# A recurrence's doubling inverse without identity products, its key norm in four columns, and sums of squares one tile behind

## The reference, cut to what matters

```python
def step(S, inp):                      # per head, state S of 64 x 64
    r_t, w_t, k_t, v_t, a_t, b_t = inp
    sa = jnp.einsum('bhij,bhj->bhi', S, a_t)
    S = S * w_t[:, :, None, :] + sa[..., None] * b_t[:, :, None, :] + v_t[..., None] * k_t[:, :, None, :]
    return S, jnp.einsum('bhij,bhj->bhi', S, r_t)
...
kk = (k * k_k).reshape(B, T, H, N)
kk = kk * lax.rsqrt(jnp.maximum(jnp.sum(kk * kk, axis=-1, keepdims=True), 1e-24))
y = wkv7_scan(r, decay, k, v, -kk, kk * a)
...
def rms_norm(x, g, eps=1e-6):
    y = x * lax.rsqrt(jnp.mean(x * x, axis=-1, keepdims=True) + eps)
    return y * g
```

## Time and profile before

| | |
|---|---|
| time, median of 3 runs | 3502.67 us (3501.64 to 3502.81) |
| the profiled execution, its own time | 3507.43 us |
| its span, first to last instruction | 3505.6 us |
| TensorE, VectorE, ScalarE, GpSimd busy | 3188.5, 1696.9, 1161.2, 142.9 us |
| mean granted clock of TensorE | 0.911 of full |
| chain that ended last: TensorE, VectorE, ScalarE, issue | 82%, 10%, 4%, 2% |

### The profile page before, as it was taken

The page is one execution under the profiler, slowest core; times in us unless marked ns, Lnnn a source line. Parts: engine busy times, 40 slices in busy tenths (PEclk is TensorE's granted clock), DMA queues, the critical chain, the costliest instruction groups (busy, mean ns, idle before and its releaser), DMA issues.

```text
span 3505.6 us, 38393 instructions
## 1 busy us (share of the span) xinstructions
PE 3188.5 (91%) x15360; PEld 2547.2 (73%) x15360; DVE 1696.9 (48%) x2759; ACT 1161.2 (33%) x1871; POOL 142.9 (4%) x145
## 2 busy tenths in 40 slices
PE   7999798888888889999999997779999879988997
PEld 6888476677777778887788885458888356877886
DVE  5434543455555554344743447755434345336235
ACT  3323133434443343233332233543223233323332
POOL 0000000112111100000000000000000000000000
PEclk9999898778776899999999998689999979997998
DMA  3333231000000033332233322013333410201231
GB/s 126 98 97 96 64 102 34 3 3 3 4 3 13 1 121 101 97 97 95 79 96 102 93 82 75 1 30 97 97 98 95 154 51 1 76 19 46 79 96 54
DMA packets 173895, 234.75 MB, mean 67 GB/s; under 512 B 14201, under 2 KB 111062, under 8 KB 173462
## 3 DMA queue, kind: packets, MB, share of 16 engines
q1 hardware_dynamic: 173718, 232.29, 21.5%
HBM read 228.05 MB, written 4.19 MB: 66 GB/s over the span
## 4 chain that ended last, share of the span: by engine, by line
PE 82%; DVE 10%; ACT 4%; issue 2%; DMA 1%; POOL 0%; SPq 0%; DVEq 0%; ACTq 0%
PE banks L796 60%; PE banks L1221 3%; PE banks L889 2%; PE banks L1215 1%; PE banks L927 1%; PE banks L951 1%; PE banks L1209 1%; PE banks L957 1%; PE banks L1161 1%; PE banks L955 1%; PE banks L901 1%; DVE diff_scores L2177 1%; DVE diff_small L2183 1%; PE banks L860 1%; PE banks L948 1%
## 5 line engine op out<-in xcount | busy, mean ns | idle before, releaser
L1756 DVE TENSOR_TENSOR weights_lo<-weights_raw,weights_hi 128x1024 fp32r<-128x1024 f32 (+2 forms) x393 | 473.1, 1207 | 1034.4 <-ACT weights_hi L1289 1033.2
L796 PE MATMUL banks<-operand_hi,weights_hi 128*128 128x512 f32 x2208 | 874.2, 396 | 35.6 <-DVE weights_lo L1756 20.9
L796 PE MATMUL banks<-operand_lo,weights_hi 128*128 128x512 f32 x2208 | 867.3, 393 | 0.0
L796 PE MATMUL banks<-operand_hi,weights_lo 128*128 128x512 f32 x2208 | 867.1, 393 | 0.0
L1289 ACT ACTIVATE weights_hi<-weights_raw 128x1024 fp32r<-128x1024 f32 (+2 forms) x393 | 407.9, 1041 | 1096.4 <-PE banks L796 1040.4
L796 PEld LDWEIGHTS banks<-operand_hi,weights_hi 128*128 128x128 f32 x2208 | 419.3, 190 | 130.9 <-issue 25.5
L796 PEld LDWEIGHTS banks<-operand_lo,weights_hi 128*128 128x128 f32 x2208 | 419.4, 190 | 89.5 <-issue 2.4
L796 PEld LDWEIGHTS banks<-operand_hi,weights_lo 128*128 128x128 f32 x2208 | 419.1, 190 | 88.8
L796 PE MATMUL banks<-hidden_ffn_hi,weights_hi 128*128 128x512 f32 x352 | 136.9, 389 | 0.0
L796 PE MATMUL banks<-hidden_ffn_lo,weights_hi 128*128 128x512 f32 x352 | 136.9, 389 | 0.0
L796 PE MATMUL banks<-hidden_ffn_mid_hi,weights_hi 128*128 128x512 f32 x352 | 136.9, 389 | 0.0
(11 more groups left out here) (517 smaller groups left out, 4700.8 us busy)
## 6 DMA issues: line engine op xcount, KB each, us to landing
weights_raw<-in_ffn_w_in_dram SPq DMA_DIRECT2D x352, 256.0 KB, 3.1
weights_raw<-in_ffn_w_out_dram SPq DMA_DIRECT2D x88, 512.0 KB, 3.7
weights_raw<-in_w_in_dram SPq DMA_DIRECT2D x36, 512.0 KB, 3.6
weights_raw<-in_rwkv_w_rkv_dram SPq DMA_DIRECT2D x24, 512.0 KB, 3.9
weights_raw<-in_w_mod_dram SPq DMA_DIRECT2D x24, 512.0 KB, 4.6
weights_raw<-in_w_kv_dram SPq DMA_DIRECT2D x16, 512.0 KB, 3.6
weights_raw<-in_rwkv_w_o_dram SPq DMA_DIRECT2D x8, 512.0 KB, 5.2
weights_raw<-in_diff_w_q_dram SPq DMA_DIRECT2D x8, 512.0 KB, 4.6
```

The costliest lines, as they stand in the source:

```text
L796: mm = nc.tensor.matmul(o, l, r, start=first and t == 0 and job["opens"], stop=last and t == 2, **skip)
L1756: nc.vector.tensor_tensor(ring_lo[0:p, u["slot"], 0:n, 0:w], ring_raw[0:p, u["ring"], 0:n, 0:w], f32(ring_hi[0:p, u["slot"], 0:n, 0:w]), A ...
```

## The change

Three things are changed.

**Inverse.** The tables of masks now contain the identity: `seed` holds minus the near pairs (the second one plus the identity), and `level` is the identity minus the old mask. GpSimd adds the identity to the first half of `L.mq` (the new event `mi`), so that the product in step `x` already contains the old inverse, and the masked product `L.xm` is the whole factor. The growth of a level is then a plain product, and all 13 identity products of an item are gone. ScalarE's copy to `L.mh` waits for `mi` instead of the masked pair. In `refine` VectorE forms twice the identity minus the product (it was ScalarE's copy), and signs move: `L.ar` is no longer negated; ScalarE and VectorE negate in copies that exist anyway.

**Key norm.** In `decay` the squares are now the stationary operand, two products with 2 moving columns each, which leaves tokens on the partitions and four numbers for each. Maximum, root and reciprocal are over four columns; VectorE then spreads them over 256 columns (`rk`), and TensorE turns the result with two transposes in the step `norm`, which wait for `rk`. VectorE's `keys` reads them from the bank.

**Sums of squares.** In the feed-forward layers, after the time mix and the attention, and after the last layer, VectorE's addition for tile k-1 (and the rest of `fed(k-1)`) stands behind the writing of tile k.

```diff
                 elif step == "decay":
                     b = bank("kk")
                     pe.wait_ge(*by_act.at(at("sq")))
-                    nc.tensor.matmul(ps[:, b, 0:HT], headsum[:, :], L.t[7], start=True,
-                                     stop=True).then_inc(*by_pe.by(at("kk")))
+                    for tb in range(2):
+                        mm = nc.tensor.matmul(ps[:, b, 2 * tb:2 * tb + 2], L.t[7][:, tb * P:(tb + 1) * P],
+                                              headsum[:, 0:P:HEAD], start=True, stop=True)
+                    mm.then_inc(*by_pe.by(at("kk")))
+                elif step == "norm":
+                    b = bank("rk")
+                    pe.wait_ge(*by_dve.at(at("rk")))
+                    for tb in range(2):
+                        mm = nc.tensor.transpose(ps[:, b, tb * P:(tb + 1) * P], L.t[7][:, tb * P:(tb + 1) * P], ident[:, :])
+                    mm.then_inc(*by_pe.by(at("rk")))
...
-                    nc.tensor.matmul(ps[:, b], identr, joined(L.inv_t), start=True, stop=False, skip_group_check=True)
                     pe.wait_ge(*by_dve.at(at(f"xm{lv}")))
                     for p in range(4):
-                        mm = nc.tensor.matmul(ps[:, b, p * P:(p + 1) * P], L.xm[:, p], L.inv_t[:, p], start=False,
-                                              stop=True, skip_group_check=True)
+                        mm = nc.tensor.matmul(ps[:, b, p * P:(p + 1) * P], L.xm[:, p], L.inv_t[:, p], start=True, stop=True)
                     mm.then_inc(*by_pe.by(at(f"t{lv}")))
                     b = bank(f"i{lv}")
-                    nc.tensor.matmul(ps[:, b], identr, joined(L.inv), start=True, stop=False, skip_group_check=True)
...
                 elif step == "norm":
                     act.wait_ge(*by_dve.at(at("n2")))
-                    nc.scalar.activation(L.t[7], L.t[7], ACT.Sqrt,
+                    nc.scalar.activation(L.sm[:, 12:16], L.sm[:, 12:16], ACT.Sqrt,
                                          bias=eps[:, EPS_NONE:EPS_NONE + 1]).then_inc(*by_act.by(at("root")))
                 elif step == "pairs":
-                    act.wait_ge(*by_dve.at(at("mq1")))
+                    act.wait_ge(*by_pool.at(at("mi")))
                     nc.scalar.activation(L.mh, L.mq[:, :, 0, :], ACT.Copy).then_inc(*by_act.by(at("mh")))
...
-                            if part:
-                                fed(k)
+                            if part and k:
+                                fed(k - 1)
+                    if part:
+                        fed(KC - 1)
...
-                    nc.vector.reciprocal(L.t[7], L.t[7]).then_inc(*by_dve.by(at("rn")))
+                    nc.vector.reciprocal(sm[:, 12:16], sm[:, 12:16]).then_inc(*by_dve.by(at("rn")))
+                    dve.wait_ge(*by_dve.at(at("rn")))
+                    nc.vector.tensor_copy(heads_(L.t[7]), sm[:, 12:16].unsqueeze(2).broadcast_to(
+                        [P, 4, HEAD])).then_inc(*by_dve.by(at("rk")))
...
+                    pool.wait_ge(*by_dve.at(at("mq1")))
+                    nc.gpsimd.tensor_tensor(L.mq[:, :, 0, :], L.mq[:, :, 0, :], i4, ALU.add).then_inc(*by_pool.by(at("mi")))
                     pool.wait_ge(*by_dve.at(at("sd1")))
                     nc.gpsimd.tensor_tensor(L.inv, f32(L.inv), i4, ALU.add).then_inc(*by_pool.by(at("inv")))
+                    pool.wait_ge(*by_pool.at(at("mi")))
                     nc.gpsimd.tensor_tensor(L.inv_t, L.mq[:, :, 0, :], seed[:, 1].unsqueeze(1).broadcast_to([P, 4, P]),
-                                            ALU.mult).then_inc(*by_pool.by(at("seed")))
-                    pool.wait_ge(*by_pool.at(at("seed")))
-                    nc.gpsimd.tensor_tensor(L.inv_t, f32(L.inv_t), i4, ALU.add).then_inc(*by_pool.by(at("invt")))
+                                            ALU.mult).then_inc(*by_pool.by(at("invt")))
```

More of the change, by code:

```diff
@@ L371, in step_of @@
                 return "d", int(use[1])
-            return {"kk": "decay", "rx": "refine", "nv": "refine", "full": "full", "w": "w", "bon": "gh", "gh0": "gh",
+            return {"kk": "decay", "rk": "norm", "rx": "refine", "nv": "refine", "full": "full", "w": "w", "bon": "gh", "gh0": "gh",
                     "gh1": "gh", "z": "z", "out": "out", "yt": "y"}[use]
@@ L376, in wkv_done @@
             act = (["za", "a", "g"] if half == 0 else []) + ["sq", "ep", "en", "ea", "root", "mh"]
-            dve = (["lw"] if half == 0 else []) + ["cs", "cl", "n2", "rn", "am", "k2", "kk", "ma", "ka", "mb",
+            dve = (["lw"] if half == 0 else []) + ["cs", "cl", "n2", "rn", "rk", "am", "k2", "kk", "ma", "ka", "mb",
                                                     "mk", "mr", "mq0", "mq1", "sd0", "sd1", "ml"]
@@ L381, in wkv_done @@
                 dve += [f"xm{lv}"] + (["nq0", "nq1"] if lv == 0 else [])
-            act += ["rx", "full", "w", "var", "std", "yl"]
-            dve += ["nv", "bonus0", "bonus", "gh0", "gh1", "z"]
+            act += ["full", "w", "var", "std", "yl"]
+            dve += ["rx", "nv", "bonus0", "bonus", "gh0", "gh1", "z"]
             dve += ["s0", "s1", "s2", "s3"] if half == 0 else ["s0", "s1", "s2"]
             dve += ["sum", "mean", "yc", "vsum", "rstd", "yn", "y1", "y"]
-            pool = ["b2", "k3", "inv", "seed", "invt", "g", "clear"] + (["sb0"] if half else [])
+            pool = ["b2", "k3", "mi", "inv", "invt", "g", "clear"] + (["sb0"] if half else [])
             return [u[0] for u in wkv_uses(half) if u[0] != "bx0"], act, dve, pool
@@ L967, in pe_program @@
                         for part in (L.mh, L.ml):
-                            mm = nc.tensor.matmul(ps[:, b, p * P:(p + 1) * P], part[:, p], L.inv[:, p], start=False,
-                                                  stop=True, skip_group_check=True)
+                            mm = nc.tensor.matmul(ps[:, b, p * P:(p + 1) * P], part[:, p], L.inv[:, p],
+                                                  start=part is L.mh, stop=part is L.ml)
                     mm.then_inc(*by_pe.by(at("rx")))
@@ L1909, in dve_program @@
             fence("rkv")
[L1910 to L1912 removed]
+            nc.vector.tensor_scalar(two_ident, ident[:, :], 2.0, None, ALU.mult).then_inc(*wkv_ready.by(0))
             dve.wait_ge(*wkv_ready.at(0))
@@ L2075, in add_and_feed @@
                                                         ALU.add).then_inc(*evac_d.by(job))
-                                add_square(stage, k, free)
+                                if k:
+                                    add_square(stage, k - 1, free)
+                            if bi:
+                                add_square(stage, KC - 1, free)
                         if bi:
@@ L2604, in tables @@
     near = (i // 2 == j // 2)
-    t["seed"] = f(np.concatenate([near & (i > j), near & (i < j)], 1))
-    t["level"] = f(np.concatenate([(i // (2 * s) == j // (2 * s)) & (i % (2 * s) >= s) & (j % (2 * s) < s)
+    unit = (i == j).astype(np.int32)
+    t["seed"] = f(np.concatenate([0 - (near & (i > j)), unit - (near & (i < j))], 1))
+    t["level"] = f(np.concatenate([unit - ((i // (2 * s) == j // (2 * s)) & (i % (2 * s) >= s) & (j % (2 * s) < s))
                                    for s in (2, 4, 8, 16, 32)], 1))
```

57 lines of the change are left out of this document (26 added, 31 removed).

## The result

The change is slower: 3545.0 us (median of 6 runs, 3530.8 to 3552.2) against 3502.7 us for the kernel before in the same comparison (6 runs, 3486.0 to 3518.5). The ratio is 1.0098, 95% interval 1.0069 to 1.0127, about 1%. The profiled execution of the change is the quickest of its six (3530.8 us, span 3528.9), so its trace shows less of the loss than the medians: 23 us of span against 42.

The account below looks back on a forecast made before the run. TensorE, 91% busy, was taken as the bound, in the recurrence in turn with short waits on other engines. Terms -63 + 19 + 17 - 8 - 1 + 9 = -27 us gave 3476 us, range 3440 to 3508.

Parts of the forecast that it names:

- Identity products: Recurrence, TensorE: removing 208 products of 128x512 against the identity, about 0.30 us each, saves 63 us.
- Key norm: Recurrence, step `norm`: TensorE newly waits before the two transposes; 1.2 us an item over 16 items, +19 us.
- GpSimd: Recurrence, before the first level: the new sum `mi` makes `inv` end later; 1.1 us an item, +17 us.
- Squares: Serial stage ends: sums of squares one tile behind shorten waits before products of ones and for weights, -8 us together.
- constants: Fewer constants and a shorter first chain: -1 us.
- The wait of 2.12 us for weights at 2119.74: TensorE waits for weights SyncE issues after the last tile is written; that tile would be written about 2 us earlier.
- The clock: Recurrence: TensorE's mean granted clock falls from 0.75 to 0.736, 479 us of busy time becoming 488, +9 us.
- My own signs of being wrong: Recurrence shorter by over 45 us or no shorter; no wait at the transposes; or a clock below 0.71.
- The third rival: Recurrence: long gaps in every item lower the clock to 0.70 instead of 0.736, 25 us more, 3501 us; chance 0.15.
- The fourth rival: Recurrence: the new wait costs its full 3.3 us in 16 items, +34, 3510 us, slower; chance 0.15.

Follow-up runs that it names:

- e2: The kernel before with the key norm alone changed, identity products kept: 3548.1 us, ratio 1.0093 to the kernel before.
- e1: The kernel before with the inverse part alone (no identity products, new tables, new GpSimd sum): 3535.5 us, ratio 1.0065 to the kernel before.
- e3: The kernel before with the sums of squares alone one tile behind: 3503.4 us, ratio 0.9969 to the kernel before.
- e11: The change with 288 discarded products ahead of the waits for key norm, square of the keys and first level: ratio 0.9771 to the kernel before.
- e6: The change with 8 discarded products ahead of each wait for the key norm, 128 in all: 3510.1 us, ratio 0.9992 to the kernel before.
- e5: The change with the norm's transposes three turns later, at step `keys`: 3520.7 us, ratio 1.0039 to the kernel before.
- e13: The kernel before with the change's squares and key norm, late transposes, identity products kept, 304 discarded products: 3411.2 us, ratio 0.9724 to the kernel before.
- e8: The kernel before with the change's squares and key norm, transposes late at step `keys`, identity products kept: 3484.2 us, ratio 0.9920 to the kernel before.
- e4: The change with a discarded 128x512 product in each of the 13 places per item of an identity product: 3550.3 us, ratio 1.0106 to the kernel before.
- e10: The change with late transposes and 160 discarded products ahead of the waits for square of the keys and first level: ratio 0.9775 to the kernel before.

## Why the prediction was wrong

Forecast 3476 us, range 3440 to 3508; measured 3545, on the other side.

- **Identity products, -63 us**: right at a constant clock. The work fell by 47 us by the product and by 51 by the clock intervals, where I counted 50, and 47 / 0.75 = 63.
- **Key norm, +19, and GpSimd, +17**: places and sizes of the waits were right (2.7 to 3.4 us at the transposes forecast, 3.1 measured; no more waits of 3.7 us at the level product). As idle time e2 shows +11 and e1 +18, the change +15: the two do not add up, and 36 was too much. For GpSimd I had kept 1.77 us for `inv`; it is 1.26, and `mi` 1.27, so `inv` should have ended hardly later. But e1's wait for GpSimd before the first level still grew by 8 us (13.0 to 21.4), and its waits at the level product by 7. In the change the wait for GpSimd is 17.9 us in 10 items, near the 2 us each that I forecast.
- **Squares -8, constants -1**: the last product of ones waits 2.24 us as forecast (2.2). From the end of the recurrence to the end of the span the three kernels without this edit take 2263 to 2267 us, the thirteen with it, the change among them, 2249 to 2261 (mean 2255), 9 us less; ahead of the recurrence it is 3 us. The whole is about -12, and e3's ratio (-11) agrees. The wait of 2.12 us for weights at 2119.74 is gone, as forecast.
- **The clock, +9: the step that failed.** "I count a fall from 0.75 to 0.736" stood on no row. Measured is 0.63, and 361 / 0.63 - 361 / 0.75 = 573 - 481 = **+92 us**. The -63, the +92 and the idle time of +15 make 44 for the stretch, measured 43; they close by the way they are reckoned, which is no test. The test is the runs with filled waits, where the clock came back and the time with it (e11 wholly, e6 in part). My own signs of being wrong were both there: a clock below 0.71 and a stretch no shorter than before.

The third rival, *the clock takes it back*, named the effect, but I priced it at 0.70 and 3501 and gave it 0.15. It rested on the long gaps, by the rule that I quoted from *TensorE: Matmul & The Clock Gate* of the Trainium skill ("HAM oscillation"). The trace agrees in kind only: every one of the 21 falls has a wait of about 1 us or more within 5 us ahead of it, and filled waits brought the clock back. But it is mostly the short waits, as told above, and e5, where the long waits for the norm are nearly gone, keeps the low clock. My argument against the rival was that half clock stands at 751 to 761 us with TensorE busy all the time and no gap near. That was a wrong reading of the trace before: a wait ends at 750.99, and the clock falls at 751.0.

```profile
750.99 1.09 PE L927 MATMUL banks<-operand_hi 128*128 128x128 f32 x4 [1.41 <-POOL operand_hi L2436]
```

Where waits were filled, such stretches all but went: 0.97 over the whole recurrence in e13. The fourth rival, *the transposes hold up the other lanes*, had the right sign. Its mechanism is real: e2 and e8 are 1.7% apart, some 61 us, 11 of which are the squares, and half of it works through the clock (0.71 to 0.77). In the change it is a part only: late transposes gave back 0.6 percentage points of the 1.0 lost, at an unchanged clock, and e5 is still slower than before.

What stays open: by what rule the clock is granted. The runs order amount, idle time and place only roughly. Why the clock, falling as often as before, returns so much later in the change is not shown, and why late transposes raise the clock where the identity products are kept (0.71 to 0.77) and not where they are out (0.63 to 0.62) was not tried.

## What to carry to other kernels

Where TensorE's granted clock is well below 1 in a stretch, work taken off it is not time won: read busy time x clock as one number and idle time as another, and price every edit at a lower clock too, before the sum is made. Look for the waits behind which the clock falls, short ones too. There the first thing to try is the opposite, to put a few discarded products ahead of these waits; here it was worth 1.1% by itself and 3% together with the change's edits, late transposes and more fillers, and only after it did the edit that removes work begin to pay. A new wait belongs as late in TensorE's list as its reader allows, behind the other lanes' work; once the waits were filled, its place no longer mattered.

## What was unexpected of the hardware

- The part with 13 products fewer in each item made the kernel slower (e1, 1.0065), and 8 useless ones more made the change faster by 1% (e6, 1.0098 to 0.9992).
- With the same 406 to 409 us of work the recurrence ran at 0.69 with discarded products beside work and at 0.81 with them ahead of two regular waits of 1 to 3 us (e4, e10). The two kernels also differ in the place of the transposes, which changed no clock between the change and e5.
- Ahead of the longest regular wait, that for the norm, fillers did little for the clock (0.63 to 0.70): 13 of these 16 waits begin at the lower level already.
- Of GpSimd's three operations of 128x512 in the step `pairs`, one takes 1.71 to 1.79 us and the others 1.25 to 1.28, in all 16 items: `inv` before, the last product in the change. The slow one runs beside VectorE's L1983 in both, but that is not the cause by itself: the change's L2447 overlaps L1983 by about as much (0.54 us, where the slow L2449 has 0.58) and takes 1.27. No run was made for it. Single instructions of the change:

```profile
759.83 1.27 POOL L2447 TENSOR_TENSOR operand_hi<-operand_hi,ident 128x512 fp32r<-128x512 f32 x1
...
761.06 1.72 POOL L2449 TENSOR_TENSOR operand_hi<-m_q,seed_masks 128x512 fp32r<-128x512 f32 x1
```

```profile
760.56 1.08 DVE L1983 TENSOR_TENSOR operand_lo<-m_q,operand_hi 128x512 fp32r<-128x512 f32 x1 [1.38 <-ACT operand_hi L1446]
```
